# Delta-rule heads on one Trainium2 core: each 128-column float32 product given as four 32-column products

## The reference

```
kk = where(strict, (k * beta) @ k.T * decay, 0)
sol = triangular_solve(kk + eye, concat([v * beta, k * beta * exp(gc)]))
u, w = sol[..., :dv], sol[..., dv:]
qk = where(causal, q @ k.T * decay, 0)

def step(state, inp):
    v_new = u_n - w_n @ state
    o = (q_n * exp(g_n)) @ state + qk_n @ v_new
    state = state * exp(g_last) + (k_n * exp(g_last - g_n)).T @ v_new
```

## Time and profile before

| what | value |
|---|---|
| median of 3 runs | 3868.53 us (3862.64 to 3874.67) |
| the profiled execution, its own time | 3872.23 us |
| its span in the profile | 3870.5 us |
| TensorE busy, share of the span | 3272.3 us, 85% |
| mean granted TensorE clock | 0.901 of full |
| the four rounds of the delta heads | 333.89 to 626.23 us from the span's start |

### The profile page before, as it was taken

How to read it: one execution, slowest core, us unless ns; L and a number is a source line. 1 busy time by engine, 2 the same in 40 slices (tenths; PEclk the granted TensorE clock), 3 DMA queues, 4 the chain that set the end, 5 groups by cost and what they waited for, 6 DMA issues and landing times. The chain is left out here.

```text
span 3870.5 us, 39759 instructions
## 1 busy us (share of the span) xinstructions
PE 3272.3 (85%) x15262; PEld 2179.7 (56%) x15262; DVE 1249.4 (32%) x1956; ACT 868.4 (22%) x1138; POOL 863.0 (22%) x387
## 2 busy tenths in 40 slices
PE   6988886799989997889996966998878888888886
PEld 3765775588767863768775954743433333333332
DVE  3524454666536003352304132743221111111112
ACT  2333223322332223242314332111100000000001
POOL 1321222233425330424341301200011111111110
PEclk8998988899999998999997955899889999999997
DMA  6324000345422330222322200202169999999996
GB/s 217 87 90 160 1 0 0 131 173 175 125 64 87 98 87 0 76 66 98 103 60 72 87 0 22 89 1 77 64 270 409 414 418 407 406 403 410 405 404 259
DMA packets 246152, 630.52 MB, mean 163 GB/s; under 512 B 18693, under 2 KB 192038, under 8 KB 221041
## 3 DMA queue, kind: packets, MB, share of 16 engines
q1 hardware_dynamic: 235249, 618.81, 42.7%
q0 software_dynamic: 10240, 8.43, 0.7%
q10 hardware_dynamic: 576, 2.10, 0.1%
HBM read 633.47 MB, written 20.97 MB: 169 GB/s over the span
## 5 line engine op out<-in xcount | busy, mean ns | idle before, releaser
L495 PE MATMUL ps<-arena_parts,arena_parts 128*128 128x512 f32 (+1 forms) x2080 | 780.8, 375 | 109.0 <-DVE arena_parts L486 38.3
L497 PE MATMUL ps<-arena_parts,ring_parts 128*128 128x512 f32 (+1 forms) x2080 | 771.1, 371 | 0.0
L382 POOL TENSOR_TENSOR ring_parts<-ring,arena_parts 128x2048 fp32r<-128x2048 f32 (+1 forms) x105 | 516.0, 4915 | 1057.4 <-ACT arena_parts L376 1057.4
L2946 PE MATMUL ps<-arena 128*64 128x512 f32 x1024 | 519.5, 667 | 159.1 <-DMA arena<-in_w_up 113.2
L496 PE MATMUL ps<-hT_parts,arena_parts 128*128 128x512 f32 (+1 forms) x1728 | 630.1, 365 | 0.0
L2947 PE MATMUL ps<-arena 128*64 128x512 f32 x1024 | 521.0, 668 | 0.0
L495 PEld LDWEIGHTS ps<-arena_parts,arena_parts 128*128 128x128 f32 x2080 | 396.5, 191 | 200.0 <-POOL ring_parts L382 56.7
L497 PEld LDWEIGHTS ps<-arena_parts,ring_parts 128*128 128x128 f32 x2080 | 396.9, 191 | 71.5
L2946 PEld LDWEIGHTS ps<-arena 128*64 128x64 f32 x1024 | 150.6, 153 | 496.2 <-issue 494.3
L496 PEld LDWEIGHTS ps<-hT_parts,arena_parts 128*128 128x128 f32 x1728 | 329.3, 191 | 51.7
L3026 DVE TENSOR_SCALAR arena<-ps 128x256 f32<-128x256 f32 x64 | 27.2, 425 | 854.5 <-PE ps L2957 854.5
(11 more groups left out here) (484 smaller groups left out, 4169.0 us busy)
## 6 DMA issues: line engine op xcount, KB each, us to landing
arena<-in_w_gate SPq DMA_DIRECT2D x64, 2048.0 KB, 18.1
arena<-in_w_up SPq DMA_DIRECT2D x64, 2048.0 KB, 22.5
arena<-in_w_down SPq DMA_DIRECT2D x64, 2048.0 KB, 23.4
ring<-in_ffn_up SPq DMA_DIRECT2D x44, 1024.0 KB, 5.1
arena<-in_ada_w SPq DMA_DIRECT2D x20, 2048.0 KB, 9.8
ring<-in_ret_w_in SPq DMA_DIRECT2D x24, 1024.0 KB, 5.4
ring<-in_ffn_down SPq DMA_DIRECT2D x16, 1408.0 KB, 7.1
ring<-in_gdn_w_in SPq DMA_DIRECT2D x16, 1024.0 KB, 5.9
```

The source lines that it names most:

```text
L382: pool.tensor_tensor(self.lower(n, kt, cols), self.slot(n, kt, cols), self.upper(room, n, kt, cols), ALU.subtract)\
L495: pe.matmul(out, upper[:, r], self.upper[r][:, part], start=(r == 0), stop=False)
L497: ins = pe.matmul(out, lower[:, r], self.upper[r][:, part], start=False, stop=(r == self.tiles - 1))
L2946: pe.matmul(k.ps[upper, 2 + u, :], m.xeT[u][:, r, :], m.w_up[u][:, r, :], start=(r == 0), stop=(r == KD - 1))
```

## The change

A helper `by_columns` gives a product as four, each with 32 of the 128 stationary columns and with its output at the partitions of those columns (0, 32, 64, 96); the moving side is the same for all four. In `DeltaHeads.tensor` the name `mm` now means that helper, so all products of the levels, of `w`, of the chunks and the key-by-key half of `gram` are given in quarters. The transposes are products with the identity, in quarters as well. `bcast` and the key-by-query half of `gram` stay whole.

```diff
+def by_columns(pe, out, lhsT, rhs, start, stop):
+
+    for q in range(0, P, P // 4):
+        ins = pe.matmul(out[q:q + P // 4], lhsT[:, q:q + P // 4], rhs, start=start, stop=stop)
+    return ins
...
     def tensor(self, pe):
         k = self.k
-        mm = pe.matmul
+        mm = lambda *of, **when: by_columns(pe, *of, **when)
...
-                mm(self.bank(lane, 0), k.ones[0:GH, :], self.gm[lane], start=True, stop=True)
-                mm(self.bank(lane, 1), k.ones[0:GH, :], self.bm[lane], start=True, stop=True).then_inc(self.sem("bcast"), 1)
+                pe.matmul(self.bank(lane, 0), k.ones[0:GH, :], self.gm[lane], start=True, stop=True)
+                pe.matmul(self.bank(lane, 1), k.ones[0:GH, :], self.bm[lane], start=True, stop=True).then_inc(self.sem("bcast"), 1)
...
-                        ins = pe.transpose(self.bank(lane, 2 + n, t), of[lane][:, chunk_at(t)], k.ident[:])
+                        ins = mm(self.bank(lane, 2 + n, t), of[lane][:, chunk_at(t)], k.ident[:], start=True, stop=True)
...
-                    ins = mm(self.bank(lane, 1, t), self.kT[lane][:, chunk_at(t)], self.tile(0, i, lane)[:, chunk_at(t)], start=True, stop=True)
+                    ins = pe.matmul(self.bank(lane, 1, t), self.kT[lane][:, chunk_at(t)], self.tile(0, i, lane)[:, chunk_at(t)], start=True, stop=True)
```

## The result

The changed kernel is slower: 3889.09 us, median of 5 runs (3881.6 to 3894.37), against 3869.07 us before (3862.64 to 3874.67); the ratio is 1.0048, with a 95% interval of 1.0034 to 1.0063. The forecast was 3863 us, 0.14% less than before; the time lies inside the stated range of 3850 to 3900, but the change went the other way, and clear of the noise.

What follows compares the result with a forecast made beforehand. TensorE, busy 85% of the span, was taken as the bound. Levels 3.2, level 0 and `w` 0.6 and chunks 1.6 make 5.4 us less: 3872.2 to 3866.8 profiled, median about 3863, range 3850 to 3900.

Steps and rivals of the forecast that it cites:

- the sum: Gains over four rounds: levels 1 to 6 3.2 us, level 0 and `w` 0.6, chunks 1.6; 5.4 us less in all.
- exposed loads: First weight load of a burst, in the open after a wait: 0.076 us less, against 0.035 more at the burst's end.
- hiding places: Idle TensorE stretches at round beginnings and the 1.96 us between rounds, taken to hide dearer transposes and tile-shape changes.
- the supply of instructions: Rival, chance 0.23: in bursts, pairs come slower than 28 ns or code is refetched each round; middle 3905 us.
- the signs it gave of being wrong: Pairs above 28 ns with issue waits, over 10 packets in later rounds with gaps, DVE waiting before L1180, level period above 6.2 us.
- a pace per pair: Load-and-product pairs in bursts, 27.3 ns needed: at 31 ns +16 us, at 35 ns +37, at 45 ns +88.
- A product in quarters, 0.218 us: Four tiles run side by side, so a product takes 0.218 us against 0.223 whole, 0.005 less.
- 0.13: Gain in us per level period: 0.09 from 20 products, plus 0.076 - 0.035 for one exposed start.
- the 5.4 us: Total gain forecast over the four rounds, from levels, `w` and chunks.
- The transposes are hidden: At round beginnings, 3.3 us more a round costs nothing behind DVE's work; rival of not hidden, 0.05, up to 3876 us.
- Changes of tile shape cost nothing: Six changes a round, 0.08 us each, fall in idle time at beginnings or between rounds; in the open 2 us or twice that.
- The clock: Rival: a shorter pause at round beginnings keeps the clock up, -8 us, 3855; chance 0.12, and 0.01 for a loss.

Runs made afterwards that it cites:

- run 2: The changed kernel with TensorE's four rounds of the heads written out instead of looped: 3874.74 us, ratio 1.0002 to the kernel before.
- run 6: The kernel before with only the levels in quarters, levels 1 to 5 as an inner loop of TensorE's program: 3869.37 us, ratio 0.9991.
- run 8: The kernel before with only the levels in quarters, written out without an inner loop: ratio 1.0019 to the kernel before.
- 11: The changed kernel with transposes whole again and levels 1 to 5 as an inner loop: ratio 1.0017 to the kernel before.
- Run 9: The kernel before with only the 16 transposes of a round as identity products in quarters: ratio 1.0001.
- Run 12: The kernel before, products whole, with two extra DVE writes at each round's start so that TensorE waits longer: ratio 1.0041.

## Why the prediction was wrong

**The step that failed** is the sum's silence on code. It counted array time, exposed loads and hiding places, put the growth of the loop's code at nothing, and set the supply of instructions aside as a rival with 0.23. That rival named the right thing, "if it no longer fits it is fetched in each round, and a late packet stops TensorE", and that is what happened: 62 packets in the heads instead of 4. Two of the signs it gave of being wrong came true, more than 10 packets in later rounds (15 and 16) and level periods above 6.2 us. But its price was built on a pace per pair, and where no packet was late the pace was not short: a burst of 192 rows takes 5.55 us, about 27.6 ns a row. The cost lies in single late packets, above all at the jump back. Runs 2, 6, 8 and 11 show it: the loss goes when the jump goes (2) or when the code fits (6), and comes with too much code whatever is in quarters (8, 11). So it is in part luck that 3889 lies inside the stated range: the range reached up to 3900 for a slow pace that did not come.

**A product in quarters, 0.218 us:** right. Between DVE's two L1200 rows at 369.56 and 371.30 TensorE gives 8 products in 1.74 us, 0.2175 each; in the kernel before, the same distance is 1.79 us (371.08 to 372.87), 0.224 each. The undisturbed level went from 6.17 to 6.07 us, inside the 6.0 to 6.1 that was stated. That is 0.10 where the sum had 0.13. A chunk takes 2.43 us (402.15 to 404.58 for DVE's update of the second lane) instead of 2.49:

```profile
402.15 0.35 DVE L1211 SCALAR_TENSOR_TENSOR hT<-hT,ps 128x128 f32<-128x128 f32 x1 [0.30 <-PE ps L330]
...
404.58 0.35 DVE L1211 SCALAR_TENSOR_TENSOR hT<-hT,ps 128x128 f32<-128x128 f32 x1 [0.31 <-PE ps L330]
```

So the gain is real where nothing eats it, if a little smaller than the 5.4 us: 0.9991 in run 6, with the levels alone, is 3 to 4 us, with an interval from 0 to 7, and part of it can be the inner loop's.

**The transposes are hidden:** right, and for the reason given. From the timeline of round 1 of the changed kernel:

```profile
340.40 5.57 PE L330 MATMUL ps<-ident,arena 128*32 128x128 f32 x128
...
345.79 1.05 PE L330 MATMUL ps<-arena 128*32 128x128 f32 x32
...
348.87 1.16 PE L1068 MATMUL ps<-arena 128*128 x8
...
351.55 0.68 DVE L1187 TENSOR_TENSOR arena<-arena,ps 128x512 f32<-128x512 f32 x1
```

They end at 345.97 and the gram products at 350.03, which is 16.75 us from the start of the round and earlier than before (351.41, 17.52 us from its start); and the old L1180 stands 18.27 us from the start of the round in both kernels. Run 9 shows it in the time.

**Changes of tile shape cost nothing:** right as far as seen, though one change costs more than the 0.08 us that was read for it. The weight loads stop for 0.20 us before each L1068, inside the same cover, and run 2 makes all the changes at no loss.

**The clock** was put down as a chance of gain. It went the other way, through something that was not in the rival: the pause between rounds, which the prediction used as a hiding place for a change of shape. Run 12 shows that making this pause longer is dear. It was costed as idle time that could be filled, and the prediction did not ask what it costs when it grows.

Of the 16.0 us, then: 5.9 are pauses after the jump (shown by 2 and 11, and by the packets that land 1.5 us before TensorE goes on). The 5.6 of the slow beginnings follow from the longer pause; run 12 and the beginnings of the other profiles support that, with one beginning of three in run 12 against it. The stops inside bursts, 7.9 us in the level periods, come with the fetch too: they are gone where the code fits, and each ends 1.35 to 1.58 us after a packet has landed. The 3.4 us that go off again are the quarters' gain with the clock of this profile. The pause after a jump differs between 2.9 and 4.4 us from kernel to kernel because its packet lands earlier or later: at 15 of the 16 joins with a fetch behind a jump TensorE went on 1.51 to 1.67 us behind it, and at one 2.02 us. Why the packets are late just there, and why two places of the round have the stops, stays open.

## What to carry to other kernels

Splitting an instruction into four inside a loop multiplies the loop's code. Count the instruction packets of one round in the profile, multiply, and compare with the largest loop that is not fetched again in later rounds, before costing the array time. If the split is worth having, make room for it first: an inner loop over levels that are alike turned a loss of 0.2% (run 8) into a time that is 0.1% below the kernel before or just equal to it (run 6, 0.9983 to 1.0000). If a wait looks too long for the engine that it is put down to, look when the last instruction packet landed. And ask of an idle stretch not only whether new work fits in, but what happens when it gets longer.

## What the runs showed of the hardware that was not expected

- A TensorE loop whose first pass took 6 packets of 16 KB was kept, with no packet in its later rounds; one of 7 (two rounds of whole products) and one of 8 were fetched again in the later passes. In the loop the fetch also brings more than the code: 62 packets against 54 for the same four rounds written out.
- At the jump back of a loop that is fetched again, TensorE waited 2.9 to 4.4 us where it had waited 1.96 for DVE, and the profile mostly still names DVE. That DVE had ended 1.97 us earlier gives it away, and so does the packet that landed 1.51 to 1.67 us before TensorE went on (2.02 at one join of 16).
- Fetched straight ahead, 13 to 14 packets in a round of 73 us cost next to nothing (1.0002), with four stops of 2.4 us in all.
- Making four pauses before a round 1.5 us longer each (3.5 instead of 2 us at the joins) cost about 16 us of 3870 by the ratio, and 10.2 us in the heads of the one profile.
- Outputs of 9 and of 32 columns, four side by side, take about the same time against 128 moving columns: 0.109 us for four of 32 (16 fours between 369.56 and 371.30), and some 0.109 by the prediction's estimate for four of 9.
